# Convolution taps divided 3 to 2 over the projection steps, and the end of the first compressed softmax put into the unit loop

## The reference, cut to what matters

```python
q, kc, vc, ks, vs, kw, vw, g_nsa, u, g_mrg = mixer_inputs(z, w_in)
o_attn, win_state = attend(q, g_nsa, kc, vc, ks, vs, kw, vw)
o_conv, conv_state = conformer_conv(u, conv_hist, conv_w, conv_b, conv_ln_g, conv_ln_b)
h = (g_mrg[:, :, 0] * (o_attn @ w_attn_out) + g_mrg[:, :, 1] * (o_conv @ w_conv_out)) @ w_out

s_c = jnp.einsum('bqgrd,bngd->bqgrn', q, kcmp)
p_c = masked_softmax(s_c, (cmp_end[None, :] <= t[:, None])[None, :, None, None, :])
o_c = jnp.einsum('bqgrn,bngd->bqgrd', p_c.astype(vcmp.dtype), vcmp)
```

## Time and profile before

| | us |
|---|---|
| median of 3 runs (lowest, highest) | 1035.48 (1034.77, 1036.06) |
| the profiled execution | 1037.45 |
| its span, first to last instruction | 1035.9 |
| PE busy | 968.2 (93%) |
| DVE busy | 567.8 (55%) |
| ACT busy | 404.2 (39%) |
| POOL busy | 203.0 (20%) |

### The profile page before, as it was taken

How to read it: one execution, slowest core, us unless ns; L and a number is a source line. 1 busy time by engine, 2 the same in 40 slices (tenths; PEclk the granted TensorE clock), 3 DMA queues, 4 the chain that set the end, 5 groups by cost and what they waited for, 6 DMA issues and landing times.

```text
span 1035.9 us, 17957 instructions
## 1 busy us (share of the span) xinstructions
PE 968.2 (93%) x6757; PEld 869.8 (84%) x6757; DVE 567.8 (55%) x1083; ACT 404.2 (39%) x725; POOL 203.0 (20%) x274
## 2 busy tenths in 40 slices
PE   4999999995899899999997899999999999999996
PEld 2899999894677558999875799999999998777774
DVE  4448596799466654333335366666666665112114
ACT  5121253343354535333125455555555554222112
POOL 6433152443243320111200011111111111000000
PEclk9999999997699976999998699999999999999998
DMA  7655543231000000332361022222222222222212
GB/s 208 151 165 194 112 88 93 71 82 42 27 3 2 2 2 10 88 86 81 125 152 53 21 81 81 81 81 81 84 85 87 86 82 82 82 77 82 82 61 91
DMA packets 111293, 83.97 MB, mean 81 GB/s; under 512 B 12995, under 2 KB 98635, under 8 KB 111177
## 3 DMA queue, kind: packets, MB, share of 16 engines
q1 hardware_dynamic: 104912, 65.64, 22.2%
q0 software_dynamic: 3904, 14.66, 5.2%
q10 hardware_dynamic: 2426, 2.98, 0.9%
HBM read 78.19 MB, written 7.18 MB: 82 GB/s over the span
## 4 chain that ended last, share of the span: by engine, by line
PE 81%; DVE 9%; issue 3%; DMA 3%; ACT 2%; POOL 1%; POOLq 0%; SPq 0%; DVEq 0%; ACTq 0%
PE ps L1444 22%; PE ps L1445 22%; PE ps L1446 22%; DVE yc L1118 5%; PE ps L1666 2%; PE ps L1511 2%; PE ps L1689 2%; PE ps L1476 2%; DMA raw<-in_w_in_dram 1%; DMA page<-in_state_kv_win_dram 1%; PE ps L1626 1%; DVE wl L1049 1%; PE ps L1559 1%; PE ps L1703 1%; PE ps L1629 1%
## 5 line engine op out<-in xcount | busy, mean ns | idle before, releaser
L1444 PE MATMUL ps<-zh,wh 128*128 128x288 f32 (+1 forms) x1264 | 377.3, 298 | 4.2 <-DVE wl L1049 2.2
L1446 PE MATMUL ps<-zh,wl 128*128 128x288 f32 (+1 forms) x1264 | 375.6, 297 | 0.0
L1445 PE MATMUL ps<-zl,wh 128*128 128x288 f32 (+1 forms) x1264 | 375.5, 297 | 0.0
L1444 PEld LDWEIGHTS ps<-zh,wh 128*128 128x128 f32 (+1 forms) x1264 | 238.7, 189 | 5.9 <-DVE wl L1049 2.7
L1445 PEld LDWEIGHTS ps<-zl,wh 128*128 128x128 f32 (+1 forms) x1264 | 238.6, 189 | 0.7
L1446 PEld LDWEIGHTS ps<-zh,wl 128*128 128x128 f32 (+1 forms) x1264 | 238.4, 189 | 0.7
L1049 DVE TENSOR_TENSOR wl<-raw,wh 128x1024 fp32r<-128x1024 f32 (+1 forms) x57 | 68.9, 1209 | 208.0 <-ACT wh L726 207.9
L726 ACT CAST wh<-raw 128x1024 fp32r<-128x1024 f32 (+1 forms) x57 | 59.0, 1035 | 294.4 <-PE ps L1446 270.8
L1118 DVE SCALAR_TENSOR_TENSOR yc<-ext,par,yc 128x64 f32<-128x64 f32 (+1 forms) x180 | 114.8, 706 | 0.0
L1006 ACT CAST wh<-raw 128x1024 fp32r<-128x1024 f32 x44 | 46.1, 1049 | 139.4 <-PE ps L1446 139.4
L687 POOL TENSOR_TENSOR hs<-cv 128x512 f32<-128x512 f32 x22 | 28.5, 1297 | 323.2 <-DVE cv L1410 323.2
(11 more groups left out here) (262 smaller groups left out, 1383.6 us busy)
## 6 DMA issues: line engine op xcount, KB each, us to landing
raw<-in_w_up_dram SPq DMA_DIRECT2D x44, 512.0 KB, 3.8
raw<-in_w_in_dram SPq DMA_DIRECT2D x30, 512.0 KB, 3.9
raw<-in_w_down_dram SPq DMA_DIRECT2D x22, 512.0 KB, 3.3
page<-in_cache_kv_dram POOLq DMA_DIRECT2D x16, 256.0 KB, 3.0
raw<-in_w_out_dram SPq DMA_DIRECT2D x7, 512.0 KB, 3.4
x<-in_x_prompt_dram SPq DMA_DIRECT2D x4, 512.0 KB, 5.8
page<-in_state_kv_win_dram POOLq DMA_DIRECT2D x16, 128.0 KB, 3.1
raw<-in_w_in_dram SPq DMA_DIRECT2D x8, 256.0 KB, 3.6
```

Source lines behind the costliest of these rows:

```text
L1444: nc.tensor.matmul(out, ah, bh, start=start, stop=False)
L1445: nc.tensor.matmul(out, ah, bl, start=False, stop=False)
L1446: return nc.tensor.matmul(out, al, bh, start=False, stop=stop)
```

## The change

Three things are changed. The taps of a convolution tile are spread over its steps with weight 3 for each step ahead of the g1 steps and weight 2 for each g1 step, in place of equal shares (`taps_by`). `cmp_norm(0)` moves on DVE from ahead of the unit loop to n = 1, behind `nmax(1)` and `rinv(0)`. The two `cmp_turn(0, ...)` move from n = 0 and 1 to n = 3 and 5 on PE and to n = 4 and 6 on DVE.

```diff
+def taps_by(s, s0):
+
+    done = sum(3 if t < S_G1 else 2 for t in range(s0, s))
+    return CW * done // (3 * (S_G1 - s0) + 2 * KT)
...
                     if s0 <= s < S_MRG:
-                        conv_taps(done, tiles, CW * (s - s0) // (S_MRG - s0), CW * (s + 1 - s0) // (S_MRG - s0))
+                        conv_taps(done, tiles, taps_by(s, s0), taps_by(s + 1, s0))
                 if s == S_GATE:
                     dve.wait_ge(cst_out, 16 * (1 + DB))
                     cmp_soft(0)
-            dve.wait_ge(gtok_ok, 2)
-            cmp_norm(0)
             for n in range(NU + 7):
...
+                if n == 1:
+                    dve.wait_ge(gtok_ok, 2)
+                    cmp_norm(0)
                 if n == 4:
                     lo(S_MRG + 1)
                 for i in range(4):
...
-                    if n == (FIRST[3 - i] - 2 if i else 0):
+                    if n == (FIRST[3 - i] - 2 if i else 4):
                         cmp_turn(i, 0)
-                    if n == (FIRST[3 - i] if i else 1):
+                    if n == (FIRST[3 - i] if i else 6):
                         cmp_turn(i, 1)
...
-                    if n == (FIRST[3 - i] - 3 if i else 0):
+                    if n == (FIRST[3 - i] - 3 if i else 3):
                         cmp_turn(i, 0)
-                    if n == (FIRST[3 - i] - 1 if i else 1):
+                    if n == (FIRST[3 - i] - 1 if i else 5):
                         cmp_turn(i, 1)
```

## The result

The changed kernel takes **1024.24 us** (median of 4 runs, 1018.33 to 1025.93) against 1035.62 of the kernel before on the same chip: a ratio of **0.9899** [0.9873, 0.9925], 11.4 us. Two repeats of both on other chips gave 0.9904 [0.988, 0.9928] and 0.9921 [0.99, 0.9943], 9.4 and 7.2 us. The forecast was 1026.8 with a range of 1023.5 to 1031.0 and a gain of 8.7, its own range 6.5 to 10.

What follows compares the result with a forecast made beforehand. DVE's tap backlog was taken to end the g1 stage; earlier taps, a shorter opening, an added 2.9 us wait and the clock's return brought values(1) 8.7 us earlier, so 1035.48 became 1026.8, range 1023.5 to 1031.0.

Steps and rivals of the forecast that it cites:

- DVE keeps step: In the g1 steps DVE's step takes 6.15 us against PE's 6.36, so the 2.2 us of `wl` waits go.
- The last run: Nine tile-taps behind `lo(27)` meet four POOL adds; the taps end at 247.7, 5.7 us earlier.
- More: Only two adds meet the last taps, or full clock returns with PE: gain 11.1 or 11.4, 1024.3 us; chance 0.15.
- The taps don't count: The taps' end stays at 253.4 and only the new order wins: gain 3.0, 1032.5 us; chance 0.05.
- The opening: At the unit loop's start, taps' end to scores(2) takes about 6.4 us; before, 9.8 to the third pair of scores.
- The added wait: Ahead of scores(3) PE idles 2.9 us, because DVE's first copy to `pcT` is queued behind `lo(28)`.
- The clock: Full clock returns some 6.5 us after PE's return at 261.05, about 267.5, giving values(1) at 270.6.
- Less: Half clock lasts 23.9 us as before, from 251.3 to 275.2: gain 4.8, 1030.7 us; chance 0.14.
- Slower: The 2.9 us idle starts a long half-clock stretch, from 261 to 288: 3.8 us slower, 1039.3 us; chance 0.03.
- The `sm` wait: With scores(1) on PE before the idle time, PE's wait for `sm` falls from 11.5 to about 6.7 us.
- The time: The median falls by 8.7 us to 1026.8; the forecast's own range is a gain of 6.5 to 10.

Runs made afterwards that it cites:

- e1_taps_only: The kernel before with only the 3 to 2 tap weights, old order at the loop's start; 1027.75 us, ratio 0.9935.
- e4_copy_at_3: The changed kernel with DVE's first copy to `pcT` at n = 3, ahead of `lo(28)`; 1023.07 us, ratio 0.9891.
- e10_lo28_late: The changed kernel with `lo(28)` and its cast at n = 10 in place of 4; 1020.90 us, ratio 0.9876.
- e3_after_again: The changed kernel unaltered, run a second time; 1024.26 us, ratio 0.9904 to the kernel before.
- e8_after_third: The changed kernel unaltered, run a third time; 1024.38 us, ratio 0.9921 to the kernel before.
- e5_weights_2to1: e4_copy_at_3 with tap weights of 2 to 1 in place of 3 to 2; 1020.23 us, ratio 0.9879.
- e6_adds_sooner: e4_copy_at_3 with ACT's products, and POOL's adds behind them, ending two steps sooner; 1018.20 us, ratio 0.986.

## Why the prediction was right

**DVE keeps step.** Both waits for `wl` are gone as said, and the g1 steps end 2.7 us earlier, counted from step 19, for 2.2 said. DVE's step of a `lo` and three tile-taps is 1.13 + 5.00 = 6.13 in the trace, for 6.15.

**The last run.** Four adds met it and it took 12.44, for the forecast's nine tile-taps and four adds, 7.9 + 4.76 = 12.66. The taps' end came 59.5 us after the start of step 19, for 59.7. *More* rested on two adds, or on a full clock as soon as PE is back; neither happened, the clock came 5.5 us after PE's return at 257.38. *The taps don't count* fell by e1_taps_only, 5.9 us of gain with the old order.

**The opening** from the taps' end to scores(2) took 6.0, for 6.4. Here the forecast added up wrongly: the terms that it names, 1.55 + 1.86 + 0.7 + 0.6 + 1.1 to 1.2 and a short `rinv(0)`, make 6.0, and that is what was measured. The 0.4 on top stands on no row.

**The added wait** on `pcT` was 2.85, for 2.9, at the place named; e4_copy_at_3 and e10_lo28_late took it away from two sides.

**The clock** was back 77.9 us after step 19 in the first profile (262.90), for 79.5: 5.5 us after PE's return where the forecast put 6.5, and 5.3 and 4.9 in e3_after_again and e8_after_third. So from scores(2) to values(1) it took 15.8 instead of 16.5. With 0.7 here, 0.4 in the opening and 0.2 of the taps, the stretch gained 10.0 for 8.7. *Less* held in one thing, the half clock lasted 23.8 us in this profile, about as long as the 23.9 before (20.5 in the two repeats). It began at 239.1, though, ahead of the idle time, where that rival put its start behind it at 251.3; counted from step 19 it began and ended over 9 us sooner than the rival had it. *Slower* needed a half clock up to 284.7, 96.7 after the start of step 19; no profile of the changed kernel comes near.

**The `sm` wait** is 4.9 in the first profile, for 6.7, and 6.6 in e8_after_third. In the first, scores(1) ran at half clock (1.65 instead of 0.92 for its first four matmuls), as did the transposes ahead of it, and so filled more of the same gap. That costs nothing, since DVE ends the gap.

**The time.** The three comparisons give gains of 11.4, 9.4 and 7.2 us, for 8.7. The first lies beyond the forecast's own 6.5 to 10, and its 1024.24 falls on the 1024.3 of *more* by chance, since nothing that *more* rested on happened. The terms of the sum were right to within 0.7 us, as the three profiles repeat; that the median of one comparison comes out as near as it does is partly luck. What the forecast didn't have is the half clock at the loop's end, which differs from one execution to another by more than any term of the sum was off.

## What to carry to other kernels

When one engine is late at the end of a stage, move its work into steps where it waits, and count what else slows it there: the adds that meet a run lengthen it, here by 4.6 us on 7.8. When an instruction is moved in a queue, look for the wait in front of its new place. And before a difference of two profiles is read as the change's work, count it between fixed points of the program and repeat one of the two, better both.

## What the runs showed of the hardware

**A collision has the same price in short and long runs.** Three tile-taps took 2.65 us with no add beside them (e5_weights_2to1, 207.25), 3.82 with one (207.73 in the changed kernel), 5.00 with two (225.63), 6.18 with three (e6_adds_sooner, 226.89): 1.17 to 1.18 per add. Nine took 7.80, 10.09 and 12.44 with none, two and four, 1.15 to 1.16 each. Between three and nine tile-taps the price is the same, so sparing taps in a stretch that keeps its adds wins only what a tile-tap takes without them, 0.87 (7.80 / 9). The Trainium skill (SBUF — State Buffer, section "Who interferes with whom") says that a VectorE instruction with two inputs in SBUF contends with a GpSimd instruction that reads SBUF. The trace agrees, with 1.15 to 1.18 us lost for each 128x576 add of some 1.8 us.

**Half clock under load.** At the end of the unit loop the clock stays at 0.51 for 28 us in which PE is busy 26.27 (e3_after_again), at 0.50 for 27.0 before, and in one profile of the changed kernel it was back after 10.2. The Trainium skill (TensorE: Matmul & The Clock Gate, section "What's actually happening") says that activity releases half speed. The stretch of 28 us speaks against that as a rule for every kind of activity; what is special in this one no run here shows. In all 14 profiles the full clock came back 2.4 to 5.6 us after the first matmul of the merge stage. In e3_after_again that matmul stands at 390.85, and from there to 395.40 PE was busy all the time at a granted clock of 0.50. In the first profile of the changed kernel the clock fell 109.4 us after values(1), some 10 later than in the two repeats (99.0 and 98.8). Whether the matmuls of the merge stage bring the clock back was not tried.
